# The adaptive modulation's matrix-vector product moved from DVE accumulations to TensorE column tiles in a two-block f32 transformer kernel

## The reference, cut to what matters

```
c_act = jax.nn.silu(c)
mod = c_act @ ada_w + ada_b                       # (1, 1024) @ (1024, 6144)
shift1, scale1, gate1, shift2, scale2, gate2 = split(mod, 6)
h = rmsnorm(x, norm1_g) * (1 + scale1) + shift1
proj = h @ w_in                                   # two attentions of 8 heads, two branch gates
x = x + gate1 * (merged @ w_out)
h2 = rmsnorm(x, norm2_g) * (1 + scale2) + shift2
x = x + gate2 * hierarchical_moe(h2, ...)         # 16 experts, 2 per token
return rmsnorm(x, final_g)
```

## Time and profile before

| | us |
|---|---|
| median of 3 runs | 865.79 |
| lowest and highest | 864.82, 865.99 |
| profiled execution, first to last instruction (span) | 862.8 |
| PE matmul busy in it | 771.7 (89%) |
| DVE busy | 448.6 (52%) |
| ACT busy | 300.8 (35%) |
| POOL busy | 273.0 (32%) |

### The profile page before, as it was taken

One profiled execution on the slowest core, in us unless ns is written; L12 is line 12 of the kernel. 1 busy time (PEld: TensorE's weight loads), 2 busy tenths in 40 slices (PEclk: granted clock), 3 DMA queues, 4 the chain that ended last, 5 costly groups with the idle time before them and its releaser, 6 DMA issues.

```text
span 862.8 us, 10202 instructions
## 1 busy us (share of the span) xinstructions
PE 771.7 (89%) x3988; PEld 536.2 (62%) x3988; DVE 448.6 (52%) x701; ACT 300.8 (35%) x531; POOL 273.0 (32%) x106
## 2 busy tenths in 40 slices
PE   1797978989999788688799999988999999999996
PEld 1587977767767666578686667766544444444432
DVE  1429996786668875779333434654421222122214
ACT  2644331544556326433244476632110011011103
POOL 0668450544436545456333333740000000000000
PEclk9999897999999889899899999998799999999999
DMA  9855684755434463258522332627999999999951
GB/s 338 301 195 174 232 283 169 290 196 195 139 147 157 161 245 128 98 196 296 203 98 98 105 128 102 225 100 287 346 338 398 396 362 389 398 395 389 398 235 49
DMA packets 91991, 202.24 MB, mean 234 GB/s; under 512 B 4272, under 2 KB 5936, under 8 KB 91824
## 3 DMA queue, kind: packets, MB, share of 16 engines
q1 hardware_dynamic: 88192, 198.19, 63.1%
q10 hardware_dynamic: 3760, 3.52, 1.3%
HBM read 200.66 MB, written 1.05 MB: 234 GB/s over the span
## 4 chain that ended last, share of the span: by engine, by line
PE 66%; DVE 22%; ACT 5%; issue 4%; ACTq 2%; POOL 1%; DMA 0%; DVEq 0%
PE psum L1009 13%; PE psum L730 10%; PE psum L731 9%; PE psum L732 9%; PE psum L1044 7%; DVE ada_acc L1519 5%; PE psum L986 4%; DVE con L1519 4%; PE psum L975 4%; DVE ring_rounded L1529 3%; PE psum L895 2%; PE psum L937 2%; ACT ring_rounded L1232 1%; PE psum L919 1%; PE psum L900 1%
## 5 line engine op out<-in xcount | busy, mean ns | idle before, releaser
L1326 POOL TENSOR_TENSOR ring_rounded<-ring,ring_rounded 128x1024 fp32r<-128x1024 f32 (+1 forms) x102 | 272.8, 2696 | 304.1 <-ACT ring_rounded L1232 303.9
L1232 ACT ACTIVATE ring_rounded<-ring 128x1024 fp32r<-128x1024 f32 (+1 forms) x136 | 134.6, 1037 | 31.0 <-PE psum L732 23.2
L730 PE MATMUL psum<-hT_rounded,ring_rounded 128*128 128x256 f32 x360 | 106.6, 296 | 7.1 <-POOL ring_rounded L1326 3.6
L731 PE MATMUL psum<-work_rounded,ring_rounded 128*128 128x256 f32 x360 | 104.5, 290 | 0.0
L732 PE MATMUL psum<-hT_rounded,ring_rounded 128*128 128x256 f32 x360 | 104.4, 290 | 0.0
L730 PE MATMUL psum<-ring_rounded,hT_rounded 128*128 128x512 f32 (+1 forms) x224 | 91.3, 408 | 12.2 <-DVE work_rounded L1422 6.0
L731 PE MATMUL psum<-ring_rounded,hT_rounded 128*128 128x512 f32 (+1 forms) x224 | 87.6, 391 | 0.0
L732 PE MATMUL psum<-ring_rounded,work_rounded 128*128 128x512 f32 (+1 forms) x224 | 87.2, 389 | 0.0
L1009 PE MATMUL psum<-ring,work 128*64 128x512 f32 x320 | 84.7, 594 | 0.0
L730 PEld LDWEIGHTS psum<-hT_rounded,ring_rounded 128*128 128x128 f32 x360 | 71.9, 200 | 9.4 <-POOL ring_rounded L1326 4.2
L1529 DVE TENSOR_TENSOR ring_rounded<-ring,ring_rounded 128x1024 fp32r<-128x1024 f32 (+1 forms) x34 | 65.4, 1923 | 15.7 <-ACT ring_rounded L1232 15.5
(11 more groups left out here) (235 smaller groups left out, 1189.7 us busy)
## 6 DMA issues: line engine op xcount, KB each, us to landing
ring<-in_w_in SPq DMA_DIRECT2D x23, 2048.0 KB, 8.1
ring<-in_expert_w_down SPq DMA_DIRECT2D x16, 2048.0 KB, 13.9
ring<-in_ada_w SPq DMA_DIRECT2D x12, 2048.0 KB, 8.1
ring<-in_expert_w_gate SPq DMA_DIRECT2D x12, 2048.0 KB, 15.2
ring<-in_expert_w_up SPq DMA_DIRECT2D x8, 2048.0 KB, 18.1
ring<-in_w_out SPq DMA_DIRECT2D x4, 2048.0 KB, 9.4
gates<-in_expert_w_up SPq DMA_DIRECT2D x4, 2048.0 KB, 20.0
hT<-in_expert_w_gate SPq DMA_DIRECT2D x4, 1024.0 KB, 15.6
```

What stands on the lines that cost most here:

```text
L730: nc.tensor.matmul(out, a[0], b[0], start=start, stop=False, skip_group_check=True)
L731: nc.tensor.matmul(out, a[0], b[1], start=False, stop=False, skip_group_check=True)
L1232: nc.scalar.activation(as_rounded(high(c)[:, piece]), src[:, piece], ACT.Copy).then_inc(chunk_hi, 1)
L1326: nc.gpsimd.tensor_tensor(as_rounded(w[:, piece]), w[:, piece], was_rounded(high(c)[:, piece]), ALU.subtract)\
```

## The change

Chunk c of the product becomes a unit "ada" on PE. The vector stands in column 0 of `c_wide[:, k, :]` (128 x 32, zeros elsewhere), as the stationary operand of 32 columns. Matmul k streams w[:, k, :] (128 x 512, f32) and writes PSUM partitions 32j to 32j+31 with j = k mod 4, so four k stand side by side in column tiles, and k and k+4 add up. Eight matmuls make a chunk. DVE copies the bank (128x512) to `ada_acc`, of which four rows are not zero, and the unit "mod" sums over the partitions as before. There is one accumulator, so ada c is evicted after mod c-1 is done. The second accumulator, its late load and four parts per chunk are gone, and "ones" is 128 wide. `some_ada` now places one whole mod and one whole ada, at twelve new places. Loads of ada chunks now count as read when their unit is done.

```diff
-    def some_ada(n):
-
-        for _ in range(n):
-            if ada:
-                c, part = ada.pop(0)
-                if ada_due and part == ADA_PARTS // 2:
-                    unit("mod", ada_due.pop(0))
-                steps.append(("ada", c, part))
-                if part == ADA_PARTS - 1:
-                    ada_due.append(c)
-            elif ada_due:
-                unit("mod", ada_due.pop(0))
+    def some_ada():
+
+        if ada_due:
+            unit("mod", ada_due.pop(0))
+        if ada:
+            ada_due.append(ada.pop(0))
+            unit("ada", ada_due[-1])
...
     for name in ("cz", "bz", "az", "ax", "cq", "ck"):
         unit("fm", name, 0)
-        some_ada(2 * (name != "cz"))
         unit("fm", name, 1)
-        some_ada(2 * (name != "cz"))
+        if name != "cz":
+            some_ada()
...
-        if n < 5 and n != 2 or entering == 1 and u[0] == "tm" and u != ("tm", "g2", 1):
-            some_ada(1)
...
                 unit("proj", br, t, half)
-                if half:
-                    some_ada(1)
+                if (t, half) == (1, 1):
+                    some_ada()
...
         unit("proj", br, 1, 0)
+        if blk == 1:
+            some_ada()
         unit("mT", blk, 0, 0)
...
     unit("wout", 1, 1, 0)
+    some_ada()
     unit("hT", 1, 0, 0)
     unit("hT", 1, 0, 1)
     steps.append(("norm_half", 1, 1))
     unit("wout", 1, 1, 1)
     steps += [("norm", 1, 1), ("norm", 2, 1)]
-
+    some_ada()
+    some_ada()
     unit("tm", "va", 0)
...
         unit(*u)
-        some_ada(2)
-    while ada or ada_due:
-        some_ada(1)
-    steps.append(("load_late",))
+        if u == ("tm", "vb", 1) or u == ("fm", "qa", 0):
+            some_ada()
+    assert not ada and not ada_due
...
-    if chunk[0] == "ada":
-        order = [s[1] for s in STEPS if s[0] == "ada" and s[2] == ADA_PARTS - 1]
-        return "dve", order.index(chunk[1]) + 1
     n = [i for i, u in enumerate(UNITS) if chunk in chunk_of(("unit",) + u)][0 if first else -1]
-    return "pe", n + 1
+    return n + 1
...
-                    who, count = last_reader(CHUNKS[n - RING])
-                    sp.wait_ge(ada_done if who == "dve" else unit_done, count)
+                    sp.wait_ge(unit_done, last_reader(CHUNKS[n - RING]))
...
+                elif kind == "ada":
+
+                    w = wait_chunk(pe, u).rearrange("p (k n) -> p k n", n=W512)
+                    if u[1] == 0:
+                        pe.wait_ge(c_ready, 1)
+                    for k in range(KD):
+                        j = k % 4
+                        last = nc.tensor.matmul(b[32 * j:32 * j + 32, :], c_wide[:, k, :], w[:, k, :],
+                                                start=k < 4, stop=k >= 4, skip_group_check=True)
...
-                for cols in (slice(P, late.start), slice(late.stop, N_CON)):
-                    act_e.dma_start(con[:, cols], a["con"][:, cols]).then_inc(con_loaded, 16)
+                act_e.dma_start(con[:, P:N_CON], a["con"][:, P:N_CON]).then_inc(con_loaded, 16)
...
-            link(v.tensor_tensor(c_act[:, :], c_tmp[:, 0, :], vec[:, VEC["c"]], ALU.mult))
+            link(v.memset(c_wide[:, :, :], 0.0))
+            v.tensor_tensor(c_wide[:, :, 0], c_tmp[:, 0, :], vec[:, VEC["c"]], ALU.mult).then_inc(c_ready, 1)
...
+                elif kind == "ada":
+                    if u[1] >= 1:
+
+                        dve.wait_ge(unit_done, UNITS.index(("mod", u[1] - 1)) + 1)
+                    last = v.tensor_copy(ada_acc[:, :], b)
...
-                        ins = v.tensor_scalar(acc, w[:, 0, :], c_act[:, 0:1], None, ALU.mult)
-                    else:
-                        ins = v.scalar_tensor_tensor(acc, w[:, k, :], c_act[:, k:k + 1], acc, ALU.mult, ALU.add)
...
```

More of the change, by code:

```diff
@@ L71 @@
 for _name, _n in (("ident", 128), ("mask_causal", 384), ("mask_swa", 384), ("mask_strict", 384),
-                  ("suffix", 128), ("before", 128), ("ones", 256), ("iota", 64), ("inv_count", 64),
+                  ("suffix", 128), ("before", 128), ("ones", 128), ("iota", 64), ("inv_count", 64),
                   ("tie", 16)):
@@ L121, in heads @@
                     steps.append((kind, g))
-    ada = [(c, part) for c in range(2 * N_MOD) for part in range(ADA_PARTS)]
+    ada = list(range(2 * N_MOD))
     ada_due = []
-    def some_ada(n):
-        for _ in range(n):
-            if ada:
-                c, part = ada.pop(0)
-                if ada_due and part == ADA_PARTS // 2:
-                    unit("mod", ada_due.pop(0))
-                steps.append(("ada", c, part))
-                if part == ADA_PARTS - 1:
-                    ada_due.append(c)
-            elif ada_due:
-                unit("mod", ada_due.pop(0))
+    def some_ada():
[4 more added lines that the diff above has]
+            unit("ada", ada_due[-1])
     steps += [("norm", 0, 0), ("norm", 0, 1)]
@@ L296, in chunk_of @@
 def chunk_of(step):
-    if step[0] == "ada":
-        return [("ada", step[1])]
+    if step[0] == "unit" and step[1] == "ada":
+        return [("ada", step[2])]
     if step[0] == "split":
@@ L421, in two_block_kernel @@
         aff = sb("aff", [P, 2, KD])
-        c_act = sb("c_act", [P, KD])
+        c_wide = sb("c_wide", [P, KD, 32])
         c_tmp = sb("c_tmp", [P, 2, KD])
@@ L487, in two_block_kernel @@
         sig_ready = sem("sig_ready")
[L488 removed]
+        c_ready = sem("c_ready")
         c_exp = sem("c_exp")
@@ L743, in wait_piece @@
             def wait_piece(n, c, q):
-                if last_reader(c, first=True)[1] == n + 1:
+                if last_reader(c, first=True) == n + 1:
                     m = SPLITS.index(c)
@@ L807, in unit @@
                     c = u[1]
-                    pe.wait_ge(con_loaded, 16 * 2)
-                    pe.wait_ge(ada_done, c + 1)
+                    pe.wait_ge(con_loaded, 16)
+                    pe.wait_ge(*evicted(("ada", c)))
                     if c // 2 in (2, 5):
-                        last = nc.tensor.matmul(b[:, :], ones[:, 0:P], ada_accs[c % 2], start=True, stop=True)
+                        last = nc.tensor.matmul(b[:, :], ones[:, 0:P], ada_acc[:, :], start=True, stop=True)
                     else:
                         for j in range(4):
-                            last = nc.tensor.matmul(b[:, j:j + 1], ada_accs[c % 2][:, j * P:(j + 1) * P], ones[:, 0:1],
+                            last = nc.tensor.matmul(b[:, j:j + 1], ada_acc[:, j * P:(j + 1) * P], ones[:, 0:1],
                                                     start=True, stop=True)
+                elif kind == "ada":
[6 more added lines that the diff above has]
+                                                start=k < 4, stop=k >= 4, skip_group_check=True)
                 elif kind == "proj":
@@ L1506, in pool @@
                 last.then_inc(pooled_ready, 1)
[L1508 to L1516, removed]
-                        ins = v.tensor_scalar(acc, w[:, 0, :], c_act[:, 0:1], None, ALU.mult)
-                    else:
-                        ins = v.scalar_tensor_tensor(acc, w[:, k, :], c_act[:, k:k + 1], acc, ALU.mult, ALU.add)
-                    if k < KD - 1:
-                        link(ins)
-                    else:
-                        ins.then_inc(ada_done, 1)
             def split_low(c, q):
@@ L1697, in _ @@
                     n += 1
-                elif s[0] not in ("begin", "split", "y_split", "sigmoid", "load_final_g", "load_late"):
-                    dict(norm_half=norm_half, split_low=split_low, y_split_low=y_split_low, fa_split=fa_split, norm=norm, ada=ada, S=probs, T=turned, V=outputs, pool=pool, mods=mods, logf=logf,
+                elif s[0] not in ("begin", "split", "y_split", "sigmoid", "load_final_g"):
+                    dict(norm_half=norm_half, split_low=split_low, y_split_low=y_split_low, fa_split=fa_split, norm=norm, S=probs, T=turned, V=outputs, pool=pool, mods=mods, logf=logf,
                          route=route, slots=slots)[s[0]](*s[1:])
```

21 lines of the change are left out of this document (5 added, 16 removed).

## The result

The changed kernel takes **904.1 us** (median of 4 runs, 903.3 to 905.1), against 865.3 (864.8 to 866.0) for the kernel before on the same chip: 1.045 times as long, 95% interval 1.0436 to 1.0465. I had forecast 904 in a range of 885 to 925. The profiled execution has a span of 901.5 us, 38.7 more than before.

What follows compares the result with a forecast made beforehand. The kernel was taken as mostly a queue on PE with holes that DVE sets. 862.8 - 56.6 + 25.2 + 69.1 = 900.5 us of span; with 3.0 to the median 903.5, said as 904, range 885 to 925.

Steps and rivals of the forecast that it cites:

- What goes away: PE's waits where DVE accumulations stand in the way, 41.1 us, and six half-clock stretches, 15.5 us, go: -56.6 us.
- wait 6: Mod 9 waits for ada 9's eviction, queued on DVE behind the residual, norm 1 1 and norm 2 1: 7.5 us.
- The ada unit: Added PE work: 12 units of 8 matmuls, four side by side, 2.1 us each, +25.2 us.
- pairs: Rival: ada's column tiles run only two at once, 3.5 us a unit; 921 us, chance 0.10.
- none at all: Rival: ada's column tiles don't run side by side, 7.0 us a unit; 963 us, chance 0.04.
- Waits 1 to 3: PE waits for the loads of ada 2, 3 and 4, released by ax, cq and ck: 7.0 us each.
- Wait 4: Load w1, now released by pa, lands late and its ACT and POOL splits hold wout 1 0 1: about 6.0 us.
- Wait 5: PE waits for ada 8's load, right behind w0's last unit and mod 7: 7.0 us.
- Wait 7: PE waits for ada 11's load, released by vb and landing behind qa and ka: 12 us.
- Slow clock: Half clock on PE behind six of the new waits, 2.6 us lost each: 15.6 us.

## Why the prediction was right, point by point

- **What goes away** (56.6; the ten items add up to 41.2, not 41.1): the accumulation waits are all gone. New waits of 65.3 us (44.6, 7.7, 6.8, 4.1 and 2.1) with a net growth of idle of 19.8 mean that 45.5 went, against my 41.1. The missing 4 are all of the 3.3 in attention (I took 2.2), 2.4 instead of 1.7 behind POOL, and two waits too short for rows 3 (1.2 for mod at L1446, 1.0 for mixed at L1436). One item was wrong in kind: the wait for hT's low part, 5.0 of the 6.0, was to be filled by ada units, but see wait 6.
- **The ada unit** (2.1 us, in ends of 1.6 to 3.5): 1.86 us from its first record to the next product at full clock, that is 22 us for twelve. The third of a microsecond for filling and draining in my 2.1 stood on no row. The full-speed work grew by 19.8, so some 2 us of PE's short pieces went elsewhere; I can't place them. The rivals "pairs" and "none at all" priced 12 x 1.4 and 12 x 4.9 more; made to happen, they are 12 x 1.7 and 12 x 5.1.
- **Waits 1 to 3** (7.0 each): 8.03, 7.42, 8.66. The place and the cause were right. I took the landing at 7.8 us, and it was 8.7, 8.0 and 9.3.
- **Wait 4**, w1 (6.0): 6.8, in one piece, at L718 behind DVE, and with a half-clock stretch of its own (1.8 us) that I had said it would cover. The late load and its splits were the cause, but not by the step that I gave. I had PE held by POOL's three quarters, and the last of these was ready at 338.57, 17.0 us after the load was issued, as forecast. PE did not wait for it. It waited for DVE, which split its own quarter from 331.48 to 334.01 and evicted after it, as the rows show:

```profile
331.48 2.53 DVE L1507 TENSOR_TENSOR ring_rounded<-ring,ring_rounded 128x1024 fp32r<-128x1024 f32 x1 [8.50 <-ACT ring_rounded L1226]
333.93 0.68 DVE L1458 TENSOR_TENSOR x_res<-psum,x_res 128x512 f32<-128x512 f32 x1
```

  What PE lacked was the bank behind that eviction, not the split itself. The order of work on DVE was missing from my account.
- **Wait 5**, ada 8 (7.0): 7.8. **Wait 7**, ada 11 (12): 12.6.
- **Wait 6** (7.5): the mod's wait is 7.7, but ada 9 itself, of which I wrote that it "needs no wait", had one of 4.1 ahead of it, for the bank that hT 1 0 1 held until DVE had evicted its low part. The same eviction held PE for 5.0 us in the kernel before, so this is the old wait moved, not filled. The 7.7 is near my 7.5 by luck. wout 1 1 1 ended at 365.8, but DVE came to its residual only at 370.79, and from there its chain took 11.3 us more. I had put the whole at 10.5 where 16 passed, and PE was idle for 11.8 of them, in the two pieces. This was my largest miss. The two rows:

```profile
370.86 3.64 PE L812 MATMUL psum<-ring,c_wide 128*32 128x512 f32 x16 [4.12 <-DVE work_rounded L1412]
382.19 1.84 PE L803 MATMUL psum<-con,ada_acc 128*128 128x1 f32 x8 [7.68 <-DVE ada_acc L1432]
```

- **Not foreseen**: 2.1 us at L839 for sig on DVE, with a half-clock stretch behind it. I had put the scan (DVE's running sum over sig) at nothing, as lying on idle DVE. It took 0.68 us before and takes 2.74 now, and the difference is as long as the wait:

```profile
424.70 0.68 DVE L1618 TENSOR_TENSOR_SCAN sig<-con,sig 8x256 f32<-8x256 f32 x1
```

```profile
461.41 2.74 DVE L1594 TENSOR_TENSOR_SCAN sig<-con,sig 8x256 f32<-8x256 f32 x1
```

  Its new operand, a broadcast one, isn't the cause: the kernel before with 12 accumulations has the old operand, and its scan took 2.76. In both slow cases POOL was splitting at the same moment, and in the fast one it had just stopped (424.39).
- **Slow clock** (15.6 for six waits): 17.9 in eight stretches. The total was near, the single stretch was not: they lose 1.3 to 5.5 us each. Over the whole trace the loss is 0.9 lower than before all the same, since two stretches of the profiled execution of before, at 47 and at 562 us (1.7 and 1.5), are not in that of after, although PE has the same short gaps there. That was no doing of the change that I can show.
- **The sum**: of span I had +37.7 and measured is +38.7. New waits are 65.3 against 53.5, the work at full clock grew by 19.8 against 25.2, the waits that went are 45.5 against 41.1, and the clock gave 0.9 back against nothing. So 12 us too little in one term meet 5, 4 and 1 in the others. The main mechanism, five ada units that wait for late loads, was as forecast in place, cause and size; ada 9's wait for its bank, PE's step in wait 4 and the scan were not. That the total is right to 1 us is luck. The median stands 2.6 us above the span, not 3.0, and 1.8 of that lies around the instructions in every execution.
- **A page's rule.** The trace of after shows a small price for a change of column width: the first ada record starts 0.21 us after the last product's (65.95 to 66.16), where products start 0.12 apart; on the way back the last group of four starts at 67.47, the next product at 68.02, 0.55 later where groups stand 0.43 apart, and the one behind it 0.22 later. That is 0.1 us going in and 0.2 coming out, for whatever reason, 0.3 a unit and under 4 us in all, 0.12 a unit of it within the 1.86. The Trainium skill (TensorEngine Tiling (Array Packing), Key Properties) has it that changing the mode drains the array. These gaps agree with it, without showing a drain as such. I had left it out of the sum as contradicted by the expert stage, and that reading was wrong. The chain can't show a gap of this kind, since it lets each piece end where the next one starts. PE's timeline before has the price there as well:

```profile
625.37 0.60 PE L1009 MATMUL psum<-ring,work 128*64 128x512 f32 x2
625.90 0.38 PE L986 MATMUL psum<-work,gates 128*128 128x128 f32 x1
```

  The first 128-column matmul starts 0.53 us after the last pair of 64 columns, where pairs stand 0.43 apart, and the one behind it 0.21 later, where the others stand 0.11 apart: 0.2 coming out, and 0.1 going in again (627.68 to 627.88). For the ada units the third of a microsecond that I had added for filling and draining covers it.

## What to carry to other kernels

Work that moves from a late reader to the head of the in-order engine turns a load's landing time into a wait: before moving it, take the load order and ask for each chunk which unit frees its slot and how much work stands between that unit and the use. Here loads that land in 8.0 to 9.3 us needed that much PE work between, and moving the loads by a place or two turned 4.5% slower into 2.6% faster. The busy share of an engine says little about what it is worth to relieve it: DVE at 52% cost 40 us, through the handful of places where PE stood behind it.

## What the runs showed of the hardware that I had not expected

- Column tiles run in f32 as well as one could wish: eight matmuls of 128 x 32 by 512 columns take 1.9, 3.6 and 7.0 us in four, two and one tiles, with four records starting within 0.02 us.
- The landing of a 2 MB load isn't one number. I took 7.8 us; the loads that PE stood waiting for in the changed kernel took 8.7, 8.0, 9.3 and 8.4, each with another load issued 0.4 us behind it, and one without such a neighbour, at 290.11 us, took 9.05, while others in both situations took 7.7 to 7.9. The kernel before had such loads too (two of ada_w issued at 112.40 and 124.79 us took 9.3 and 9.1), and I had read only the one pair. The second of a pair of 2 MB landed 5.3 to 5.5 us after the first in the changed kernel, 5.4 in the pair of rows 6. What makes the difference stays open.
- Half clock at a gap isn't a fixed price: 1.69 us of idle had a stretch at it and 1.80 did not, and two gaps of 4.1 and 7.7 us with little work between them kept the clock down for 20.5 us. With all loads reordered the same two gaps had stretches of 3.4 and 10.2 us, with full clock between them.
- Some of DVE's work takes far longer beside a split on POOL. The scan of 8x256 took 2.74 us beside one and 0.68 without. The eviction of hT's low part (128x512, L1412) took 2.47 us beside one (363.03) and 0.69 without (370.12), in one trace. The residual's eviction from PSUM took 0.68 either way (333.93 and 370.79). No run changes POOL alone, so this is read from the traces and not tested.
